# Two layers on one core: four gate chunks as two pairs with seven-product groups, and two attention breaks per pair of heads

## What is computed

```python
def first_block(x, meta_tokens, ...):            # 16 meta tokens + 256 tokens
    hn = rmsnorm(h, pre_norm_g)
    proj = einsum('bld,dc->blc', hn, w_in)       # 2048 -> 6656 columns
    qa, ka, va, ga, qb, kb, vb, gb = split(proj, ...)   # 1024 256 256 1024 1024 1024 1024 1024
    ya = gqa_axial_mixer(qa, ka, va, ...) * silu(ga)    # 8 heads of 128, rmsnorm and rope on q, k; 2 kv heads
    yb = diff_attn_mixer(qb, kb, vb, ...) * silu(gb)    # 8 heads, each softmax(s1) - lam * softmax(s2)
    y = concatenate([ya, yb]) @ w_out
    return (h + rmsnorm(y, post_norm_g))[:, 16:]

def second_block(x, ...):
    z = rms_norm(x, norm_mix) @ w_in_2           # q, k, v of 16 heads of 64; pooling branch; two gates
    y_a = chunked_rel_attention(q, k, v, rel_bias)
    ...                                          # branches, w_out_2, SwiGLU of 5632, final norm
```

## Time and profile before

| | |
|---|---|
| device time, median of 3 runs | 1713.37 us (1713.28 to 1713.53) |
| device time of the profiled execution | 1713.16 us |
| its span | 1711.4 us |
| TensorE (PE) busy | 1699.8 us, 99% |
| VectorE (DVE) busy | 1333.7 us, 78% |
| ScalarE (ACT) busy | 994.8 us, 58% |
| GpSimd (POOL) busy | 165.1 us, 10% |
| HBM | 189 GB/s read over the span |
| mean granted clock of TensorE | 0.999 |

### The profile page before, as it was taken

How to read it: one execution, slowest core, us unless ns; L and a number is a source line. 1 busy time by engine, 2 the same in 40 slices (tenths; PEclk the granted TensorE clock), 3 DMA queues, 4 the chain that set the end, 5 groups by cost and what they waited for, 6 DMA issues and landing times.

```text
span 1711.4 us, 23107 instructions
## 1 busy us (share of the span) xinstructions
PE 1699.8 (99%) x8587; PEld 1429.6 (84%) x8587; DVE 1333.7 (78%) x1637; ACT 994.8 (58%) x1394; POOL 165.1 (10%) x184
## 2 busy tenths in 40 slices
PE   9999999999999999999999999999999999999998
PEld 9998878888788887888888888888888888888887
DVE  6555765478666668767878767999999999999997
ACT  6334566556553444556555566666666676676663
POOL 1004363000000015000000000011001001001100
PEclk9999999999999999999999999999999999999999
DMA  9754434355686545455655566688688769769871
GB/s 323 241 168 140 148 124 147 124 167 187 200 265 192 171 148 155 160 170 206 200 186 188 201 211 204 226 257 256 246 233 260 249 201 290 249 204 274 253 259 65
DMA packets 200147, 348.70 MB, mean 204 GB/s; under 512 B 6912, under 2 KB 59776, under 8 KB 199552
## 3 DMA queue, kind: packets, MB, share of 16 engines
q1 hardware_dynamic: 187328, 324.21, 56.2%
q0 software_dynamic: 9936, 19.40, 6.2%
q10 hardware_dynamic: 2800, 3.96, 0.7%
HBM read 321.34 MB, written 2.10 MB: 189 GB/s over the span
## 4 chain that ended last, share of the span: by engine, by line
PE 91%; DVE 5%; issue 1%; ACT 1%; POOL 1%; POOLq 0%; DVEq 0%; ACTq 0%
PE acc L1157 6%; PE acc L1159 6%; PE acc L1158 6%; PE acc L828 6%; PE acc L830 6%; PE acc L829 6%; PE acc L884 5%; PE acc L1383 4%; PE acc L1385 4%; PE acc L1384 4%; PE acc L1397 4%; PE acc L1398 4%; PE acc L1399 4%; PE acc L885 3%; PE acc L872 2%; PE acc L873 2%
## 5 line engine op out<-in xcount | busy, mean ns | idle before, releaser
L2155 ACT ACTIVATE whi<-raw 128x1024 fp32r<-128x1024 f32 x330 | 341.9, 1057 | 153.1 <-PE acc L1385 58.7
L2869 DVE TENSOR_TENSOR wlo<-raw,whi 128x1024 fp32r<-128x1024 f32 x330 | 392.4, 1217 | 33.8 <-ACT whi L2155 32.3
L2240 DVE TENSOR_TENSOR wlo<-raw,whi 128x1024 fp32r<-128x1024 f32 x193 | 240.9, 1251 | 184.4 <-ACT whi L1685 183.9
L1685 ACT ACTIVATE whi<-raw 128x1024 fp32r<-128x1024 f32 x193 | 202.6, 1057 | 130.2 <-PE acc L885 53.9
L2728 DVE TENSOR_TENSOR wlo<-raw,whi 128x1024 fp32r<-128x1024 f32 x137 | 165.5, 1222 | 62.8 <-ACT whi L2034 61.9
L2034 ACT ACTIVATE whi<-raw 128x1024 fp32r<-128x1024 f32 x137 | 143.4, 1059 | 110.4 <-PE acc L1159 71.0
L884 PE MATMUL acc<-hboth,whi 128*128 128x512 f32 x384 | 135.8, 398 | 0.0
L1397 PE MATMUL acc<-whi,fhi 128*128 128x512 f32 x320 | 124.7, 390 | 0.1
L1399 PE MATMUL acc<-whi,flo 128*128 128x512 f32 x320 | 124.5, 389 | 0.0
L1398 PE MATMUL acc<-wlo,fhi 128*128 128x512 f32 x320 | 124.5, 389 | 0.0
L885 PE MATMUL acc<-hboth,wlo 128*128 128x256 f32 x384 | 106.8, 278 | 0.0
(11 more groups left out here) (494 smaller groups left out, 4088.1 us busy)
## 6 DMA issues: line engine op xcount, KB each, us to landing
raw<-w_in SPq DMA_DIRECT2D x112, 1024.0 KB, 5.3
raw<-w_gate_up SPq DMA_DIRECT2D x88, 1024.0 KB, 7.3
raw<-w_down SPq DMA_DIRECT2D x44, 1024.0 KB, 5.3
raw<-w_out SPq DMA_DIRECT2D x32, 1024.0 KB, 5.3
xres<-down POOLq DMA_DIRECT2D x36, 512.0 KB, 9.6
raw<-w_branch_a SPq DMA_DIRECT2D x8, 1024.0 KB, 5.2
raw<-w_branch_b SPq DMA_DIRECT2D x8, 1024.0 KB, 7.4
fcopy<-fprod SPq DMA_DIRECT2D x9, 512.0 KB, 8.8
```

The costliest lines, as they stand in the source:

```text
L1685: nc.scalar.activation(whi[:, g % 4], raw[:, j // 2, 2 * (j % 2):2 * (j % 2) + 2, :], ACT.Copy).then_inc(hi_ready, 1)
L2155: nc.scalar.activation(ring(x, odd)[0], raw_piece(u, half), ACT.Copy).then_inc(hi_ready, 1)
L2240: nc.vector.tensor_tensor(wlo[:, g % 4], raw[:, j // 2, 2 * (j % 2):2 * (j % 2) + 2, :], whi[:, g % 4].bitcast(F32), ALU.subtract).then_in ...
L2869: nc.vector.tensor_tensor(lo, raw_piece(UNIT[what, r], half), hi.bitcast(F32), ALU.subtract).then_inc(lo_ready, 1)
```

## The change

**Block one.** Blocks 9 and 10 (gates ga0, ga1) become pair p = 0 and 11 and 12 (gb0, gb1) pair 1. The order of block one from B8,4 on (B8,j is piece j of block 8): B8,4 a B8,5 v1 B8,6 v2 B8,7 b v3 c v4, then L2 to L7, R2, R3, then R4 a R5 v1 R6 v2 R7 b v3 c v4 of the next pair, then L2 to L7, R2 to R7. These are 110 entries; 104 of them carry a step as before (all but a, v3 and v4), so that B8,4 is step 68, B8,5 69, v1 70, B8,6 71, v2 72, B8,7 73, b 74, c 75, L2 to L7 76 to 81, R2 82, R3 83, R4 84, R5 85, v1 86, R6 87, v2 88, R7 89, b 90, c 91, L2 92. Product v1 is put in an aux bank, which is free again when ScalarE has kept it (`x_keep`). Evictions of blocks 8 and 10 go by tile, tile 0 ahead of c's step on ScalarE, tile 1 behind hi of v4; those of 7, 9 and 11 stand in steps 66, 84 and 100. Queries are transposed at steps 72 (both groups of qa0), 82 and 84, and scores 16, 18, 20 and 22 wait for the takes. VectorE makes the sums of the rows of x in step 60 and their lo in step 64. The third gate product moves from step 99 to 101. The load of x into `xres` goes behind four of the loads of the output projection, and waits for product v4 of pair 1, as the pairs' buffers lie in its place.

**Block two.** Both items' transposes now stand in one break, six steps after the even item's start, and the attend at eight: two breaks per pair. A third buffer of probabilities is added, and part one of an item from the fourth on waits until the transposes of the item three before it are copied.

```diff
+X_ENTRY = ("a", "v1", "v2", "b", "v3", "c", "v4")
+X_STEPS = ("v1", "v2", "b", "c")
+Q_X = 9
+
+
+def x_entry(between, p):
+
+    order = []
+    for key, own in zip(between, X_ENTRY):
+        order += [key, ("pair", p, own)]
+    return order + [("pair", p, op) for op in X_ENTRY[len(between):]]
+
+
+X_SEQ = x_entry([("block", Q_X - 1, j) for j in range(4, 8)], 0) + [("pair", 0, ("L", n)) for n in range(2, 8)]
+X_SEQ += [("pair", 0, ("R", n)) for n in (2, 3)] + x_entry([("pair", 0, ("R", n)) for n in range(4, 8)], 1)
+X_SEQ += [("pair", 1, (side, n)) for side in "LR" for n in range(2, 8)]
+SEQ1 = [("block", n // 8, n % 8) for n in range(8 * Q_X - 4)] + X_SEQ
+X_PLACE = {key: n for n, key in enumerate(SEQ1)}
+X_STEP = {}
+for key in SEQ1:
+    if key[0] == "block" or isinstance(key[2], tuple) or key[2] in X_STEPS:
+        X_STEP[key] = len(X_STEP)
+assert len(X_STEP) == 8 * Q_WOUT
+MORE_X = len(SEQ1) - 8 * Q_WOUT
+W_PLACE = {key: len(SEQ1) + n for n, key in enumerate(W_SEQ)}
+MORE = len(W_SEQ) - 32 + MORE_X
+
+
...
+EVICT_STEPS = {(8, 2): 7, (10, 4): 9, (12, 4): 11}
 START1, START2 = 43, 8 * 21 + 6
+QUERY_STEPS = {(9, 0): ((7, 0), (7, 1)), (10, 2): ((8, 0),), (10, 4): ((8, 1),)}
...
 
 def turn_step(n):
 
-    return start_of(n) + (6 if n < ITEMS1 else 4)
+    return start_of(n) + (6 if n < ITEMS1 or n % 2 == 0 else 4)
 
 
 def attend_step(n):
 
     if n >= ITEMS1:
-        return start_of(n) + 5
+        return start_of(n) + (8 if n % 2 == 0 else 6)
     return start_of(n) + (8 if is_b(n) and n < 15 else 7)
...
-GATE_STEPS = ((11, 6), (12, 2), (12, 3))
+GATE_STEPS = ((11, 6), (12, 2), (12, 5))
...
-            if n < ITEMS1 and n % 3 == 2:
-                return pbuf3
-            return pbuf[:, n % 3 if n < ITEMS1 else n % 2]
+            if n % 3 == 2:
+                return pbuf3 if n < ITEMS1 else pbuf4
+            return pbuf[:, n % 3]
...
+                if n in (16, 18, 20, 22):
+                    pe.wait_ge(qk_taken, 3 + (n - 16) // 2)
...
+            def x_piece(p, op):
+
+                g = x_did(p, op) - 1
+                u = use_of(Q_X + 2 * p)
+                if op == "a":
+                    pe.wait_ge(*use_taken(u - 2))
+                if op == "v2":
+                    pe.wait_ge(x_seeded, p + 1)
+                if op == "v3":
+                    pe.wait_ge(x_corrected, 2 * p + 1)
+                if op == "c":
+                    pe.wait_ge(x_right, p + 1)
+                if op == "v4":
+                    pe.wait_ge(x_corrected, 2 * p + 2)
+                pe.wait_ge(lo_ready, g + 1)
+                if op == "v1":
+                    if p == 0:
+                        pe.wait_ge(xs_ready, 1)
+                    bank = aux_bank()
+                    pair_part(g, bank, sum_of(xshi, xslo, 0), 0, start=True, counted=True)
+                    aux_used(("v1", p), (x_kept, p + 1))
+                    return
+                pair_product(g, op, acc[u % 2], acc[(u + 1) % 2], x_stat, xshi, xslo)
...
+                if key in X_STEP:
+                    before_step(X_STEP[key] // 8, X_STEP[key] % 8)
+                if key[0] == "block":
+                    block_piece(key[1], key[2])
+                else:
+                    x_piece(key[1], key[2])
+
+
...
+            for q in range(2, Q_X):
                 c0 = W1[q][2] * CW
                 if q in HALVED:
                     halved_block(q, w1, c0)
                 else:
                     quad(q, column_block(w1, c0))
-                if q == 3:
-                    sp.dma_start(xres[:], t["x"][0].rearrange("(i p) d -> p i d", p=P)).then_inc(xres_in, 16)
+            for p in range(2):
+                sides = {"L": column_block(w1, W1[Q_X + 2 * p][2] * CW), "R": column_block(w1, W1[Q_X + 2 * p + 1][2] * CW)}
+                for m, (side, r) in enumerate(PAIR_LOADS):
+                    if m >= 4:
+                        sp.wait_ge(lo_ready, x_did(p, PAIR_LAST[m - 4]))
+                    else:
+                        sp.wait_ge(lo_ready, x_did(0, PAIR_LAST[m + 4]) if p else X_PLACE["block", Q_X - 1, 2 * m + 1] + 1)
+                    sp.dma_start(raw[:, m % 4], sides[side][r].rearrange("(k p) n -> p k n", p=P)).then_inc(raw_in[m % 4], 16)
...
+                    if (p, m) == (0, 3):
+                        sp.wait_ge(piece_used, x_did(1, "v4"))
+                        sp.dma_start(xres[:], t["x"][0].rearrange("(i p) d -> p i d", p=P)).then_inc(xres_in, 16)
...
+            def evict1(b, tiles=range(TT)):
+
+                act.wait_ge(piece_used, x_done(b))
+                if b == 7:
+                    act.wait_ge(rstd1, 1)
+
+                what = W1[b][0]
+                dst = tmp if b in (9, 11) else stg
+                if b == 9:
+                    act.wait_ge(roped, 7)
+                if b >= 11:
+                    act.wait_ge(gated, b - 10)
+                for i in tiles:
+
+                    done = nc.scalar.activation(dst[:, i, :], acc[use_of(b) % 2][i][:], ACT.Silu if what == "gb" else ACT.Copy,
+                                                scale=ss[:, i:i + 1])
+                done.then_inc(evicted if 1 in tiles else first_evicted, 1)
...
+                for block, half in QUERY_STEPS.get((b, j - 1), ()):
+                    h = 4 * (block - 7) + 2 * half
+                    take(("t", block, half), qta[:, h:h + 2, :], CW)
...
+            def x_hi(p, op):
+
+                g = x_did(p, op) - 1
+                m, half = pair_home(op)
+                if op in ("a", "c") or half == 0 and m > 1:
+                    act.wait_ge(raw_in[m % 4], 16 * (Q_X + 2 * p + m // 4 + 1))
+                if op in ("v1", "v2", "v3", "v4"):
+                    act.wait_ge(x_sums, 4 * p + {"v1": 1, "v3": 2, "v2": 3, "v4": 4}[op])
+                act.wait_ge(piece_used, g - 3)
+                nc.scalar.activation(whi[:, g % 4], pair_raw(op), ACT.Copy).then_inc(hi_ready, 1)
+
+            def x_seed_left(p):
+
+                act.wait_ge(piece_used, x_did(p, "a"))
+                left = acc[use_of(Q_X + 2 * p) % 2]
+                nc.scalar.activation(left[1], left[0], ACT.Copy).then_inc(x_seeded, 1)
+
+            def x_keep(p):
+
+                act.wait_ge(piece_used, x_did(p, "v1"))
+                if p:
+                    act.wait_ge(x_corrected, 2 * p)
+                else:
+                    act.wait_ge(xs_ready, 1)
+                nc.scalar.activation(xq5[:], aux[(use["v1", p] - 1) % 2][:], ACT.Copy).then_inc(x_kept, 1)
+
+            def x_seed_right(p):
+
+                act.wait_ge(x_corrected, 2 * p + 1)
+                act.wait_ge(first_evicted, p + 1)
+                nc.scalar.activation(acc[use_of(Q_X + 2 * p + 1) % 2][0], xless[:], ACT.Copy).then_inc(x_right, 1)
+
+            done_op = None
+            for key in SEQ1:
+                kind, n, op = key
+                b, j = divmod(X_STEP[key], 8) if key in X_STEP else (None, None)
+                if b == Q_WOUT - 1 and j in (4, 5):
+                    stat_group(G_Y + j - 4)
+                if kind == "block":
+                    split(n, op)
+                else:
+                    x_hi(n, op)
+                if done_op is not None and done_op[1] == "v1":
+                    x_seed_left(done_op[0])
+                if done_op is not None and done_op[1] == "v2":
+                    x_keep(done_op[0])
+                done_op = (n, op) if kind == "pair" else None
+                if kind == "pair" and op == "c":
+                    evict1(Q_X - 1 + 2 * n, (0,))
+                if kind == "pair" and op == "v4":
+                    x_seed_right(n)
+                    evict1(Q_X - 1 + 2 * n, (1,))
+                if b is not None:
+                    act_step(b, j)
...
+                if n >= ITEMS1 + 3:
+                    dve.wait_ge(pt_ready, n - 2)
...
+                if (b, j) == (7, 4):
+                    sums_of_rows(xrows, xhi, xlo, xraw).then_inc(xs_raw, 1)
+                if (b, j) == (8, 0):
+                    dve.wait_ge(xs_hi, 1)
+                    nc.vector.tensor_tensor(xslo[:], xraw[:], xshi[:].bitcast(F32), ALU.subtract).then_inc(xs_ready, 1)
...
+            def x_lo(p, op):
+
+                g = x_did(p, op) - 1
+                dve.wait_ge(hi_ready, g + 1)
+                nc.vector.tensor_tensor(wlo[:, g % 4], pair_raw(op), whi[:, g % 4].bitcast(F32), ALU.subtract).then_inc(lo_ready, 1)
+
+            def x_sum(kind, p):
+
...
+            def x_without_u2(p):
+
+                dve.wait_ge(piece_used, x_did(p, "v2"))
+                dve.wait_ge(x_kept, p + 1)
+                if p:
+                    dve.wait_ge(x_right, p)
+                nc.vector.tensor_tensor(xless[:], xq5[:], acc[use_of(Q_X + 2 * p) % 2][1], ALU.subtract).then_inc(x_corrected, 1)
+
+            def x_without_u3(p):
+
+                dve.wait_ge(piece_used, x_did(p, "v3"))
+                dve.wait_ge(evicted, EVICTED[Q_X - 1 + 2 * p])
```

(25 more changed lines are left out.)

364 lines of the change are left out of this document (184 added, 180 removed).

## The result

The changed kernel takes 1731.49 us (median of 4 runs, 1730.58 to 1734.37) beside 1713.32 (median of 4) for the kernel before: ratio 1.0109, 95% interval 1.0092 to 1.0127, or 18.2 us more. The forecast was 1722.6, with a range up to 1728. The direction is right, the size half of what came. The profiled execution took 1730.58 us, its span is 1728.5, 17.1 over the span of before. The two main things to read in it are ten idle times of TensorE, and two stretches with a low clock.

The account below looks back on a forecast made before the run. TensorE, busy 99% of the span, was taken as the bound. Gains of −4.9 and eight new waits of +14.15 gave +9.2 on 1713.16: 1722.4, or 1722.6 at the median's level; 8 in 10 range 1711 to 1728.

Parts of the forecast that it names:

- R3: Rival, chance 0.08: TensorE's clock falls after a rest of 3 to 4 us, about 2.6 each: 1725 to 1728.
- the old waits: Two TensorE waits in the kernel before, 0.71 us at query transposes and 0.47 at 284.72, forecast to go: −1.18.
- (a) to (g): Seven new TensorE waits in block one, steps 59 to 90, in order +0.5, +2.35, +3.9, +1.8, +1.6, +0.8, +1.8 us.
- (c): New TensorE wait at step 75, scores of item 16, behind a chain from block 8's tile 0 eviction: +3.9 us.
- (g): New wait at step 90, item 20's attend waiting for copies behind the eviction of block 10's tile 0: +1.8 us.
- (h): New wait at step 91, for a bank behind the third part in step 92, 7.9 against 6.4: +1.4 us.
- (b): New TensorE wait at step 73, scores of item 15, a chain of 4.95 us against 2.6 of TensorE: +2.35.
- the bounds of +0.3 and −2.4: Block two's seven removed breaks, taken as −1.0 us: at most a gain of −2.4 or a loss of +0.3.
- R5: Rival without its own chance: block two's merge gives nothing, bound by VectorE and ScalarE, +1.0 us on any case.
- R1: Rival, chance 0.12: the leads cover the new waits, only the +0.5 at step 59 is left: 1709 us.
- R2: Rival, chance 0.15: new waits feed each other, only about 5 us of the 14 are paid: 1713.5, no change.
- R4: Rival, chance 0.05: VectorE's passes lengthen, some 0.5 us each, by GpSimd's traffic or xres's 2 MB: 1726 to 1728.

Follow-up runs that it names:

- filler_clean: Changed kernel with TensorE multiplying zeros in all four long waits, item 20's ahead of the attend's bank, zeros set in step 63: 1727.95 us.
- take_late: Changed kernel with ScalarE taking the queries two steps behind their transposes instead of one: 1724.27 us.
- evict_behind: Changed kernel with tile 0 of blocks 8 and 10 evicted behind the attention of c's step instead of ahead of it: 1727.37 us.
- bias_early: Changed kernel with VectorE's part one of items 12 to 15 two steps behind the scores instead of three: 1724.14 us.
- sums_behind: Changed kernel with VectorE's sums for v2 and v4 behind their step's attention instead of ahead of it: 1727.63 us.
- best2: Changed kernel with take_late, sums_behind, item 15's part one earlier, tile 0 between copies and exps, x's row sums later, item 20's third part after c's attention: 1715.19 us.
- filler: Changed kernel with TensorE multiplying zeros at two waits, 16 matmuls at item 16's scores and 8 at item 20's attend: 1733.06 us.
- tuned: Changed kernel with bias_early, take_late, evict_behind, and the third part of items 16 to 20 one step behind the attend instead of two: 1724.67 us.

## Why the forecast held in direction and failed in size

The step that failed is the adding up of the costs. The sum prices each wait at the difference of two chains and has no term for what comes with a wait. The largest term that it lacks is the clock, which it has only as rival R3, with a chance of 0.08 and as another case than the forecast. It is not another case: it follows from a wait that I forecast with 0.60, and comes on top of it. The prediction names the sign itself, a dip between 240 and 330 us, and it came at 268. The falls cost 3.2 us in the profiled execution. `filler_clean` shows it: with the four long waits filled, 3.5 us are back. It is also what carries the time out of the range, since `filler_clean`, at 1727.95, lies just inside it. Priced as R3 prices it, twice 2.6 on top of the forecast's own 1718 to 1727, the range would have ended near 1732. But `filler_clean` is still 5.4 over the forecast. Most of that part is two waits not seen, a longer (h), 0.15 beside each wait, and 2.0 elsewhere, less what block two gained.

- The products and the old waits: 12 matmuls fewer and both waits gone, as forecast. Their −2.73 and −1.18 are the forecast's own figures; plain pieces of block one start a matmul every 0.231 us and not 0.2275, which changes the first by 0.05.
- The waits (a) to (g) were each within 0.1 us of the forecast. take_late, evict_behind, bias_early and sums_behind show that they are what I took them for: each moves one kind of instruction in one engine's order, and the waits that my chain held it for fall by nearly its length. That (c) fits to 0.07 is in part luck: lo took 1.38 from start to start and bias 0.94, where I had 1.15 and 0.8, the evictions were a little shorter, and the chain of 7.9 instead of 7.7 is offset by the 0.17 that the idle time does not list. The terms that I wrote down for (g) add up to 1.9 and not 1.8, those for (h) to 1.5 and not 1.4.
- (h) 1.4 became 2.11. My chain ran through the eviction; in fact VectorE's correction behind v3 stands ahead of the third part. evict_behind leaves the 2.11 as it is, best2 puts the third part ahead and leaves 0.74.
- Two waits I did not see at all, 0.83 and 0.45, in step 69 and at v1. The first is part one of item 12, which stands behind the sum for v2 in VectorE's order; I had counted that sum as free. sums_behind removes it. The second is a third part that the bank of v1 waits for, a piece sooner than an attend or transposes would.
- The idle time that a row lists is 0.15 us less than what a wait costs: 1.5 us over ten. I added no such term.
- R3's size: a fall cost 1.6 us twice here and 2.9 behind (b) in `filler`; the 2.6 of the estimate lies between.
- Block two: −1.0 by estimate, −1.8 by the run, inside the bounds of +0.3 and −2.4. I had taken the break's start alone; the stretch is not bound by VectorE and ScalarE (R5 is refuted).
- R1 and R2 are refuted: the waits did not pay for each other.
- R4 came in part, and beside the forecast, too. Of the added sums six took 1.22 us, the others 1.31 and 1.48; but the lo pass at 234.45 took 2.33, and some in (c)'s neighbourhood 1.39 to 1.45. From start to start the pass at 234.45 and the sum at 238.10 took 2.25 and 1.40, where passes otherwise start 1.14 apart (230.94 to 232.08): 1.37 us in VectorE's unbroken order, more than the 0.83 that TensorE then waited. The memory was still (3 GB/s), GpSimd was busy throughout (3.00 of 3 us), so of R4's two causes the traffic of GpSimd is the one that fits. It isn't shown: it was busy 2.92 of 3 us in the kernel before too, where the pass at 233.90 took 1.38, and no run takes its work away. The 2 MB of xres left no wait behind.
- The third gate product moves two steps, not the three that the prediction says; nothing hangs on it.

9.2 + 1.8 (waits) + 1.5 + 3.2 − 0.7 (block two) + 2.0 (entry of the output projection, breaks, not placed) = 17.0, the difference of the spans. The median of the changed kernel lies another 0.9 over its profiled run.

## What to carry to other kernels

Seven products of half a piece's length, in place of four pieces, save one matmul in eight, and they also halve the time in which the other engines may answer. Write the chain from each TensorE instruction to the next one that waits for it, in the other engines' order, before counting what the matmuls give. A wait that is forecast at several microseconds is to be priced with its clock, in the same case. And an instruction moved ahead in an in-order engine helps only if what it waits for is done by then: by `tuned`'s trace, third parts one step too early cost more than they freed.
